# Memory cross attention: the query product's last two pieces by column tile, two heads' scores ahead of its last tile

## The reference

```python
def memory_cross_attention(h, m, w_q, w_kv, w_o):
    B, S, _ = h.shape
    q = (h @ w_q).reshape(B, S, XA_HEADS, XA_HEAD_DIM)
    k, v = jnp.split(m @ w_kv, 2, axis=-1)
    ...
    s = jnp.einsum('bqhd,bkhd->bhqk', q, k).astype(jnp.float32) * (XA_HEAD_DIM ** -0.5)
    p = jax.nn.softmax(s, axis=-1).astype(v.dtype)
    o = jnp.einsum('bhqk,bkhd->bqhd', p, v).reshape(B, S, XA_WIDTH)
    return o @ w_o
...
        x = x + memory_cross_attention(rmsnorm_2(x, norm_xattn[l]), rmsnorm_2(mem, norm_mem[l]),
                                       w_xq[l], w_xkv[l], w_xo[l])
    return rmsnorm_2(x, final_norm)
```

## Time and profile before

| | us |
|---|---|
| median of 3 runs | 1678.84 (1678.31 to 1679.32) |
| the profiled execution | 1679.67 |
| its span (first to last instruction) | 1677.6 |
| PE busy | 1645.3 (98%) |
| DVE busy | 1005.1 (60%) |
| ACT busy | 876.4 (52%) |

### The profile page before, as it was taken

One profiled execution on the slowest core, in us unless ns is written; L12 is line 12 of the kernel. 1 busy time (PEld: TensorE's weight loads), 2 busy tenths in 40 slices (PEclk: granted clock), 3 DMA queues, 4 the chain that ended last, 5 costly groups with the idle time before them and its releaser, 6 DMA issues.

```text
span 1677.6 us, 28637 instructions
## 1 busy us (share of the span) xinstructions
PE 1645.3 (98%) x11182; PEld 1502.2 (90%) x11182; DVE 1005.1 (60%) x1433; ACT 876.4 (52%) x1262; POOL 21.8 (1%) x46
## 2 busy tenths in 40 slices
PE   8999999999999999999999999989999999999996
PEld 8989998879999999999998888878998888898895
DVE  5566657556666666666664444474666455776555
ACT  6355557446555545545553444353533696655545
POOL 3000000000000000000000000010000000000000
PEclk9999999999999999999999999999999999999998
DMA  7654541554555566656565665555565557555551
GB/s 230 201 162 139 162 134 46 190 173 146 189 187 189 193 200 200 199 190 195 191 214 177 206 200 182 185 156 155 173 178 174 164 150 237 178 185 177 176 189 63
DMA packets 154575, 295.11 MB, mean 176 GB/s; under 512 B 13428, under 2 KB 15624, under 8 KB 153592
## 3 DMA queue, kind: packets, MB, share of 16 engines
q1 hardware_dynamic: 153512, 289.76, 55.0%
q0 software_dynamic: 944, 4.14, 0.7%
q10 hardware_dynamic: 32, 0.01, 0.0%
HBM read 291.51 MB, written 2.10 MB: 175 GB/s over the span
## 4 chain that ended last, share of the span: by engine, by line
PE 96%; DVE 2%; ACT 1%; issue 0%; DMA 0%; ACTq 0%; SPq 0%; DVEq 0%
PE bank L1525 30%; PE bank L1527 29%; PE bank L1526 29%; PE upper L1667 1%; PE upper L1670 1%; ACT junk L526 1%; PE upper L1684 1%; PE upper L1800 1%; PE bank L1581 1%; DMA x_tok<-in_x 0%; PE upper L1581 0%; PE upper L1697 0%; PE upper L1698 0%; PE upper L1844 0%; PE upper L1696 0%
## 5 line engine op out<-in xcount | busy, mean ns | idle before, releaser
L909 DVE TENSOR_TENSOR w_lo<-raw,w_hi 128x1024 fp32r<-128x1024 f32 (+1 forms) x548 | 654.2, 1208 | 530.6 <-ACT w_hi L468 529.0
L468 ACT ACTIVATE w_hi<-raw 128x1024 fp32r<-128x1024 f32 (+1 forms) x548 | 568.3, 1049 | 572.3 <-PE bank L1527 566.6
L1525 PE MATMUL bank<-hT_hi,w_hi 128*128 128x256 f32 x2208 | 614.1, 278 | 0.7 <-DVE hT_lo L940 0.7
L1526 PE MATMUL bank<-hT_lo,w_hi 128*128 128x256 f32 x2208 | 611.4, 277 | 0.0
L1527 PE MATMUL bank<-hT_hi,w_lo 128*128 128x256 f32 x2208 | 611.3, 277 | 0.0
L1525 PEld LDWEIGHTS bank<-hT_hi,w_hi 128*128 128x128 f32 x2208 | 414.8, 188 | 1.9 <-issue 1.1
L1526 PEld LDWEIGHTS bank<-hT_lo,w_hi 128*128 128x128 f32 x2208 | 415.4, 188 | 0.0
L1527 PEld LDWEIGHTS bank<-hT_hi,w_lo 128*128 128x128 f32 x2208 | 415.0, 188 | 0.0
L1525 PE MATMUL bank<-w_hi,hT_hi 128*128 128x512 f32 x672 | 265.0, 394 | 0.0
L1527 PE MATMUL bank<-w_hi,hT_lo 128*128 128x512 f32 x672 | 261.8, 390 | 0.0
L1526 PE MATMUL bank<-w_lo,hT_hi 128*128 128x512 f32 x672 | 261.5, 389 | 0.0
(11 more groups left out here) (359 smaller groups left out, 1167.8 us busy)
## 6 DMA issues: line engine op xcount, KB each, us to landing
raw<-in_w_in SPq DMA_DIRECT2D x180, 512.0 KB, 3.8
raw<-in_w_up SPq DMA_DIRECT2D x176, 512.0 KB, 4.5
raw<-in_w_down SPq DMA_DIRECT2D x80, 512.0 KB, 4.7
raw<-in_w_out SPq DMA_DIRECT2D x64, 512.0 KB, 4.5
raw<-in_w_xkv SPq DMA_DIRECT2D x16, 512.0 KB, 4.7
raw<-in_w_down SPq DMA_DIRECT2D x16, 256.0 KB, 2.9
raw<-in_w_xq SPq DMA_DIRECT2D x8, 512.0 KB, 3.8
raw<-in_w_xo SPq DMA_DIRECT2D x8, 512.0 KB, 4.3
```

What stands on the lines that cost most here:

```text
L468: act.activation(w_hi[:, s, at:at + n], raw[:, s, 0:n], ACT.Copy).then_inc(hi_ready, 1)
L909: dve.tensor_tensor(w_lo[:, s, at:at + n], raw[:, s, 0:n], w_hi[:, s, at:at + n].bitcast(F32), ALU.subtract).then_inc(lo_ready, 1)
L1525: pe.matmul(o, l_hi, r_hi, start=start, stop=False, skip_group_check=True)
L1526: pe.matmul(o, l_hi, r_lo, start=False, stop=False, skip_group_check=True)
```

## The change

The query product's first six pieces stay as they were. PE then waits for both last pieces at once and goes column tile by column tile: tile 0 of pieces 6 and 7, tile 1, tile 2, the scores of heads 0 and 1, tile 3, the scores of heads 2 and 3. Two new semaphores go with it: `xq_first` (after tile 1, lets ACT copy the first bank) and `xq_copied` (1 for ACT's copy, 1 for DVE's; the scores of heads 0 and 1 wait for 1, those of 2 and 3 for 2). The two copies no longer count in `banks_free`, and `evacuated(g)` is 2 lower from `xq` on.

DVE puts its copy between max 0 and max 1, and max 2 ahead of norm 0. ACT does all exponentials first, and the copies of the transposes after them. Both move the split of one piece (the third of `xo`) from the end of the query group to behind the attention.

```diff
         def evacuated(g, off=0):
 
-            return 2 * (g + 1) + off
+            return 2 * (g + 1 - (g >= GROUP["xq"][0])) + off
...
             g = GROUP["xq"][0]
-            group(g, side=x_side, take=lambda: copy_out(mix2[:, 0, 0:W], g))
+            group(g, side=x_side, early=True)
+            act.wait_ge(xq_first, 1)
+            act.activation(mix2[:, 0, 0:W], out_of(g, 0), ACT.Copy).then_inc(xq_copied, 1)
...
-            x_exps(0)
-            x_exps(1)
-            x_exps(2)
+            for h in range(XA_HEADS):
+                x_exps(h)
             x_probs(0)
-            x_exps(3)
             x_probs(1)
+            x_probs(2)
             x_out_hi(0)
-            x_probs(2)
+            x_probs(3)
             x_out_hi(1)
-            x_probs(3)
             x_out_hi(2)
             x_out_hi(3)
+            split(FIRST_PIECE[g] + 7 + SLOTS - 1)
             warm(4, ACT.Sqrt)
...
             x_max(0)
+            dve.wait_ge(mm_done, FIRST_PIECE[g + 1])
+            dve.tensor_copy(mix2[:, 1, 0:W], out_of(g, 1)).then_inc(xq_copied, 1)
             x_max(1)
+            x_max(2)
             x_norm(0)
-            x_max(2)
+            x_max(3)
             x_norm(1)
-            x_max(3)
             x_norm(2)
             x_norm(3)
...
             x_out_lo(3)
+            split(FIRST_PIECE[g] + 7 + SLOTS - 1)
...
-            group(GROUP["xq"][0], "T", a_hi=xT_hi, a_lo=xT_lo, first=6, side=x_side)
-            pe.wait_ge(banks_free, evacuated(GROUP["xq"][0]))
-            for h in range(XA_HEADS):
+
+            def x_scores(h):
+                pe.wait_ge(xq_copied, h // 2 + 1)
                 for b in range(NB):
...
                 ins.then_inc(xs_done, 1)
+
+            g = GROUP["xq"][0]
+            group(g, "T", kcs=(2,) * 6, a_hi=xT_hi, a_lo=xT_lo, first=6, side=x_side, more=True)
+            u, pair = FIRST_PIECE[g], 2 * (g % 2)
+            pe.wait_ge(lo_ready, u + 8)
+            for ft in range(4):
+                for j in (6, 7):
...
+                    if ft == 3:
+                        ins.then_inc(mm_done, 1)
+                if ft == 1:
+                    ins.then_inc(xq_first, 1)
+                if ft == 2:
+                    x_scores(0)
+                    x_scores(1)
+            x_scores(2)
+            x_scores(3)
```

More of the change, by code:

```diff
@@ L271, in build @@
         x_factors = sem("x_factors")
+        xq_first, xq_copied = sem("xq_first"), sem("xq_copied")
         out_scaled0, out_scaled, stored, x_gained = sem("out_scaled0"), sem("out_scaled"), sem("stored"), sem("x_gained")
@@ L468, in split, with group @@
                 act.activation(w_hi[:, s, at:at + n], raw[:, s, 0:n], ACT.Copy).then_inc(hi_ready, 1)
-            def group(g, i=None, step=0, side=None, take=None):
+            def group(g, i=None, step=0, side=None, take=None, early=False):
                 u, n = FIRST_PIECE[g], PLAN[g][1]
-                for j in range(n):
+                for j in range(n - early):
                     split(u + j + SLOTS - 1, i, step)
@@ L477, in group @@
                         side(j - 1)
+                if early:
+                    return
                 if side and not take:
@@ L1467, in _ @@
             g = GROUP["xq"][0]
-            group(g, side=x_side, take=lambda: copy_out(mix2[:, 1, 0:W], g))
+            for j in range(7):
+                split(FIRST_PIECE[g] + j + SLOTS - 1)
+                if j:
+                    x_side(j - 1)
             def x_max(h):
@@ L1527, in three, with group @@
                 return pe.matmul(o, l_lo, r_hi, start=False, stop=stop, skip_group_check=True)
-            def group(g, mode, i=None, step=0, kcs=(2,) * 8, a_hi=hT_hi, a_lo=hT_lo, first=None, chunks=False, heads=False, side=None):
+            def group(g, mode, i=None, step=0, kcs=(2,) * 8, a_hi=hT_hi, a_lo=hT_lo, first=None, chunks=False, heads=False, more=False, side=None):
                 u = FIRST_PIECE[g]
@@ L1536, in group @@
                 k = 0
-                total = sum(kcs)
+                total = KC if more else sum(kcs)
                 for j, n in enumerate(kcs):
@@ L1913, in _ @@
                 ins.then_inc(xs_done, 1)
+            g = GROUP["xq"][0]
[4 more added lines that the diff above has]
+                for j in (6, 7):
+                    at = place(u + j)
+                    hi, lo = wide(w_hi, (u + j) % SLOTS, 2, W, at), wide(w_lo, (u + j) % SLOTS, 2, W, at)
+                    for c in range(2):
+                        ins = three(bank[pair + ft // 2][:, ft % 2 * S:(ft % 2 + 1) * S], hi[:, c, ft * P:(ft + 1) * P],
+                                    lo[:, c, ft * P:(ft + 1) * P], xT_hi[:, 2 * j + c, :], xT_lo[:, 2 * j + c, :],
+                                    False, 2 * j + c == KC - 1)
+                    if ft == 3:
[7 more added lines that the diff above has]
+            x_scores(3)
             def x_turn(h):
```

## The result

The changed kernel takes 1684.63 us (median of 7 runs, 1683.05 to 1687.44) against 1678.31 (7 runs, 1676.21 to 1679.32) before. The ratio is 1.0043, with a 95% interval of 1.0033 to 1.0053: slower, by 7.2 us (5.5 to 8.9). The forecast was 1684.7, in a range from 1682.9 to 1687.3.

The account below looks back on a forecast made before the run. PE, 96% of the chain of work, was taken to bound the kernel. 0.3 + 2.24 + 1.55 + 1.55 + 0.3 = 5.9 us on 1678.84 gave 1684.7 us; own range 1683.4 to 1686.0, with rivals 1682.9 to 1687.3.

Parts of the forecast that it names:

- part 3: Output product `xo`: groups 1 to 3 each wait for the previous group's adds, costing 2.24, 1.55 and 1.55 us.
- restarts: Output product: the first matmul after each of three waits runs slower, 0.1 us each, bounds 0 and 0.2.
- Part 1: Query product's end: tile order costs nothing, ACT's copy is hidden, two heads' early scores add 1.86 us.
- Part 2: Attention, from the query product's end to `xo`: 1.57 us shorter; with the early scores, `xo` starts 0.3 us later.
- X: The query product's end, forecast to move from 1632.05 to 1633.91; the attention's steps are counted from it.
- B: Stretch from DVE's copy to the output product's first matmul; 12.16 us before, with `xo` forecast at X+10.62, the copy at X+0.03.
- Rival 1: PE's clock falls to half speed in a gap, mainly in `xo`: 1.65 us more per fall, 1686.4 for one; chance 0.27.
- Rival 2: Output product: something else brings `banks_free` to 120 before group 0's adds, so PE isn't held; 1679.1 us, chance 0.06.
- Rival 3: Attention: max 3 need not wait for norm 0, so values 0 start 0.8 us sooner; 1683.9 us, chance 0.09.
- A: Stretch from the query product's first matmul to DVE's copy, 23.29 us before; the tile order was priced at nothing, 0 to 0.3.

Follow-up runs that it names:

- e1: The changed kernel with `group`'s wait on `banks_free` taking the adjusted count, so each output group waits only for the group two before; 1678.82 us, ratio 1.0004 to before.
- e2: The kernel before, with output groups 1 to 3 also waiting until the group right before them is added onto x; 1683.31 us, ratio 1.0031.
- e5: On top of e4, all scores behind tile 3, those of heads 0 and 1 waiting for ACT's copy alone, DVE's copy ahead of max 0; 1676.85 us, ratio 0.9989.
- e4: On top of e1, norm 0 ahead of max 2 on DVE and first transposes' copies ahead of the last exponentials on ACT; 1676.84 us, ratio 0.9993 to before.
- e3: The changed kernel with small unused matmuls ahead of output groups 1 (twelve), 2 and 3 (eight each); 1685.49 us, ratio 1.0040 to before.
- e6: On top of e4, only head 0's scores ahead of tile 3, and norm 0 ahead of max 1; 1676.33 us, ratio 0.9992 to before.
- e7: On top of e4, small unused matmuls ahead of turn 0 (four), turn 1 (six) and values 0 (two) in the attention; 1676.30 us, ratio 0.9990 to before.

## Why the prediction was right

The step that decides, part 3, held: the wait, its releaser and its price. PE waited three times for DVE's adds because the two counts taken out of `banks_free` were not taken out of `group`'s wait. e1 removes the loss with that line, e2 makes it in the kernel before. The forecast terms were 2.24, 1.55 and 1.55, and 0.1 for each of three restarts, 5.64 in all. Measured without the slow clock the starts are 2.18, 1.66 and 1.67 further apart and the last group's end 0.14, which is 5.65 with the restarts in it. The first wait was put a little too high and the restarts too low. The first wait is longer by 0.61 than in e2, where 0.69 was worked out for the moved split; the rows show the adds right behind the delayed splits, and in e1, where nobody waits for them, they also come 6.50 after the product's start instead of 5.86.

Part 1: two heads' scores cost 1.79 instead of 1.86. The new accumulation order cost nothing: e5, which has it without the early scores, takes 23.30 to DVE's copy, against 23.29 before. ACT's copy was over 0.56 us ahead of the scores.

Part 2: values 0 came 6.17 after DVE's copy; worked out was 6.16 (X+6.19 with the copy at X+0.03). B is 10.51 against 10.59, so parts 1 and 2 together are +0.14 instead of +0.3. That norm 0 stands behind max 2 fits as the reason: e4 undoes it, and the exponentials' order with it, and gains 1.02; how much of this is norm 0's is not shown.

Rival 1 is real in kind: the clock fell behind the first wait in the profiled execution and cost 1.6 us, where 1.65 was worked out for one fall. How often the clock falls there stays open, since one execution of each kernel is profiled; e3 does not settle it. The sentence of the Trainium skill weighed there (TensorE: Matmul & The Clock Gate, "Loop structure matters more than you think") speaks of matmuls that follow immediately, and e1 agrees: there VectorE adds one group while PE runs the next without a wait, and the clock is 1.00 over the output product. It does not cover matmuls that have to wait for the adds: there the clock was 0.50 behind a 1.99 us wait in the changed kernel, and 1.00 behind its two waits of 1.38 us and the three of e2.

That 1684.63 lies on the forecast to 0.1 us is partly luck. The forecast starts from 1678.84 for the kernel before, and the runs beside the result gave 1678.31, so the change is 6.3 us by the medians and 7.2 by the ratio, not 5.9 (the ratio's interval, 5.5 to 8.9, holds both). And the execution of 1684.63 has the fall of the clock in it, which the forecast leaves out; the 2.44 us by which it came sooner to the query product more than make up for that. What bears the prediction out is the stretch itself: 5.8 us without the clock, where 5.9 were worked out.

The same 2.44 us upset a sign that counts from the span's start. The output product was to begin between 1643.7 and 1645.3 and began at 1641.94, which by the prediction's words would speak against part 2; 2.44 later it is 1644.38, inside. The lower end of the forecast's own range, 1683.4, is 0.3 under what its bounds add up to (0.5 earlier, 5.34 of waits, no restarts: 1683.7).

Rival 2, that PE isn't held, was wrong; its time, 1679.1, is what e1 shows once the count is adjusted (1678.82). Rival 3 would have needed the attention 0.8 us shorter than worked out; from DVE's copy to the output product it was 0.08 shorter, and max 3 did follow norm 0 by 0.61 us (1634.34 to 1634.95), as worked out.

## What to carry to other kernels

When a copy stops counting in a semaphore that others read by constants, go through all waits on it, also those that don't use the helper that was changed: a wait that is two counts too strict changes no result as long as the count still comes, and shows only as a new row among the waits (here 4.8 us). Two pairs of banks bring nothing if the second may start only when the first is empty: the groups then start 7.1 us apart instead of 5.4.

An early result is worth only what the queues of the next engines let through: give the early heads' next step (their norm) its place ahead of work that isn't there yet. Here the scores did not have to be early at all: e5 gets an equally short stretch (34.40 us) from copying the finished bank early and letting the first scores wait for that copy alone.

## What the runs showed of the hardware

- Twelve matmuls in a row that accumulate into the same 256 columns of a bank ran as fast as the old order: A is 23.30 us in e5 and 23.29 before.
- The granted clock fell to 0.50 in different places in executions of kernels whose instructions there are the same: in the attention in e2 and not in before; in e3 and not in e1, with the same attention. In e2 the waits of PE just ahead of it were 0.55, 0.94 and 0.27 us, and the kernel before has the same three and kept 1.00. So the waits alone don't tell whether the clock falls. Each of these falls (the changed kernel's in the output product too) cost 1.4 to 1.7 us. This is more than the differences between the medians of e4, e5, e6 and e7, which is why those are read from stretches of the timeline, and a third or more of the scatter of the kernel before (1676.15 to 1680.4).
